# Hybrid RG-LRU / attention / expert-choice step on one core: input weights by column blocks, expert lists from two sorted halves, weight rests in smaller pieces

## What is computed

```python
def _recurrent_mixer(xn, w_in, ...):            # layer 0
    gate, u = jnp.split(xn @ w_in, 2, axis=-1)
    u = _centred_dwconv(u, conv_w, conv_b)
    h = _linear_scan(a_f, b_f, h0_f) + flip(_linear_scan(a_b, b_b, h0_b))
    y = (h * jax.nn.gelu(gate)) @ w_out

def _expert_choice_moe(xn, w_router, w_gate, w_up, w_down):
    aff = jax.nn.softmax(xt @ w_router, axis=-1)
    g, idx = lax.top_k(aff.T, cap)              # cap = 64 latent, 16 context
    xe = xt[idx]
    h = jax.nn.silu(xe @ w_gate) * (xe @ w_up)
    ye = (h @ w_down) * g
    out = zeros.at[idx].add(ye)

# each of the six vectors of a layer (shift, scale, gate for mixer and experts):
m = silu(cond) @ mod_w[layer] + mod_b[layer]
```

## Time and profile before

| | before |
|---|---|
| median of 3 runs (lowest to highest) | 1864.85 us (1864.16 to 1870.14) |
| profiled execution: its own time | 1864.11 us |
| profiled execution: span | 1862.3 us |
| busy share PE, DVE, ACT, POOL | 89%, 33%, 20%, 17% |
| traffic | 524.99 MB, mean 282 GB/s |

### The profile page before, as it was taken

One profiled execution on the slowest core, in us unless ns is written; L12 is line 12 of the kernel. 1 busy time (PEld: TensorE's weight loads), 2 busy tenths in 40 slices (PEclk: granted clock), 3 DMA queues, 4 the chain that ended last, 5 costly groups with the idle time before them and its releaser, 6 DMA issues.

```text
span 1862.3 us, 30729 instructions
## 1 busy us (share of the span) xinstructions
PE 1659.7 (89%) x13351; PEld 771.2 (41%) x13351; DVE 614.3 (33%) x1137; ACT 370.4 (20%) x770; POOL 312.1 (17%) x358
## 2 busy tenths in 40 slices
PE   4799859479999999999879788794799999999997
PEld 0688647123333333332258666472233333333322
DVE  2467675510111121010267567556101111210102
ACT  2377741100000000000151355411000000000000
POOL 1133230210101110110020167301101011101110
PEclk8899979689999999999989899896899999999999
DMA  9400553989999999999920200315899999999993
GB/s 390 146 1 1 214 224 119 410 335 404 382 405 410 399 407 414 401 404 405 336 85 1 96 24 24 137 79 216 313 405 381 403 410 399 405 415 398 407 356 115
DMA packets 57934, 524.99 MB, mean 282 GB/s; under 512 B 12607, under 2 KB 12895, under 8 KB 25038
## 3 DMA queue, kind: packets, MB, share of 16 engines
q1 hardware_dynamic: 48096, 490.62, 64.9%
q0 software_dynamic: 8176, 27.08, 5.2%
q10 hardware_dynamic: 1534, 5.38, 0.7%
HBM read 500.50 MB, written 22.55 MB: 281 GB/s over the span
## 4 chain that ended last, share of the span: by engine, by line
PE 77%; DVE 9%; DMA 5%; ACT 5%; issue 2%; POOL 1%; SPq 0%; DVEq 0%; POOLq 0%; ACTq 0%
PE ps L912 36%; PE ps L916 18%; PE ps L855 6%; PE ps L1170 5%; DMA W<-x_hat,gi_c 2%; DMA ring<-in_mod_w 2%; DMA ring<-in_rg_w_in 1%; PE ps L1218 1%; PE ps L1192 1%; PE ps L1205 1%; PE ps L939 1%; PE ps L1077 1%; PE ps L954 1%; PE ps L759 1%; ACT W L1426 1%
## 5 line engine op out<-in xcount | busy, mean ns | idle before, releaser
L912 PE MATMUL ps<-ring,W 128*32 128x512 f32 x4608 | 552.4, 597 | 4.0 <-issue 2.6
L916 PE MATMUL ps<-ring,W 128*16 128x512 f32 x2304 | 300.2, 593 | 0.0
L912 PEld LDWEIGHTS ps<-ring,W 128*32 128x32 f32 x4608 | 145.9, 110 | 335.1 <-issue 333.0
L1241 ACT ACTIVATE W<-ps 128x512 f32<-128x512 f32 (+5 forms) x137 | 72.0, 542 | 910.5 <-PE ps L954 707.7
L1738 DVE TENSOR_TENSOR W<-ps,amod 128x1024 f32<-128x1024 f32 (+1 forms) x32 | 28.5, 892 | 487.4 <-PE ps L939 366.2
L912 PE MATMUL ps<-over_rows,W 128*32 128x512 f32 x1536 | 182.7, 593 | 0.0
L916 PEld LDWEIGHTS ps<-ring,W 128*16 128x16 f32 x2304 | 67.6, 97 | 177.3 <-issue 177.3
L1747 DVE TENSOR_TENSOR W<-ps,W 128x1024 f32<-128x1024 f32 x16 | 19.6, 1225 | 278.1 <-PE ps L916 278.1
L916 PE MATMUL ps<-over_rows,W 128*16 128x512 f32 x768 | 99.9, 592 | 0.0
L855 PE MATMUL ps<-wo_hl,mo_hi 128*128 128x512 f32 x320 | 89.7, 403 | 5.3 <-DVE mo_lo L1652 5.3
L912 PEld LDWEIGHTS ps<-over_rows,W 128*32 128x32 f32 x1536 | 48.1, 110 | 108.3 <-issue 107.8
(11 more groups left out here) (282 smaller groups left out, 2189.0 us busy)
## 6 DMA issues: line engine op xcount, KB each, us to landing
ring<-in_moe_w_down SPq DMA_DIRECT2D x52, 2048.0 KB, 11.7
ring<-in_moe_w_up SPq DMA_DIRECT2D x48, 2048.0 KB, 13.4
ring<-in_moe_w_gate SPq DMA_DIRECT2D x44, 2048.0 KB, 11.3
ring<-in_mod_w SPq DMA_DIRECT2D x48, 1024.0 KB, 11.3
over_rows<-in_moe_w_gate SPq DMA_DIRECT2D x20, 2048.0 KB, 11.1
over_rows<-in_moe_w_up SPq DMA_DIRECT2D x16, 2048.0 KB, 11.8
over_rows<-in_moe_w_down SPq DMA_DIRECT2D x12, 2048.0 KB, 12.9
ring<-in_rg_w_in SPq DMA_DIRECT2D x8, 1024.0 KB, 27.5
```

The source lines that it names most:

```text
L912: nc.tensor.matmul(ps[q * CG:(q + 1) * CG, bank + n, :], lat(q, k), expert_slots(slots[q // 2], 1)[:, 0, cols], start=(k == 0), stop=(k == ...
L916: mm = nc.tensor.matmul(ps[q * CG:q * CG + CC, bank + 2, :], ctx(a, k), expert_slots(slots[a], 1)[:, 0, h * D + n * 512:h * D + (n + 1) * ...
L1241: nc.scalar.activation(out, in_, ACT.Copy).then_inc(done, n)
```

## The change

- **Opening.** `rg_w_in` is laid out by column blocks, so that slot b holds both column blocks b. SP loads tokens, vectors 1 and 0, then blocks 0 to 3, the small recurrent weights `bd`, and blocks 4 to 7. Vector 2's weights come behind them into slots 0 to 3 and vector 3's into 4 to 7, each slot free once `column_rest` has read it; vector 4's come into slots 0 to 3 once PE has used vector 2's. PE multiplies vectors 2 and 3 together at the last feature block, and 4 behind it; the three are turned together.
- **Mixer output.** PE does the products with high weights of tiles 0 and 1 first, then the weight rests of tile 0, the gate rows, the weight rests of tile 1. In layer 0 ACT makes all 8 high parts between vector 4 and `mo_hi`, and DVE all 8 rests behind the token rests; POOL none.
- **Attention.** POOL splits `at_w_o` in quarters of 128x256: behind every unit from 2 to 34 one high part and one rest.
- **Lists.** The 512 latent tokens are two halves on separate partitions, sorted together in 8 rounds over 256 columns. Merging: the k-th of the first half against the (64-k)-th of the second, the larger of each pair belongs to the best 64. POOL waits for the first 4 lists (indices) instead of 10. An extra exponential of one element stands ahead of the softmax on ACT.

```diff
-MOD_SLOT = {0: 0, 1: 4, 2: 8, 3: 0, 4: 4, 5: 8, 6: 0, 7: 4, 9: 8, 10: 0, 8: 0, 11: 8}
+MOD_SLOT = {0: 8, 1: 4, 2: 0, 3: 4, 4: 0, 5: 8, 6: 0, 7: 4, 9: 8, 10: 0, 8: 0, 11: 8}
...
+        def in_columns(n):
+            return ring[:, n // 2, (1 - n % 2) * D:(2 - n % 2) * D].rearrange("p (k j) -> p k j", k=KB)
...
-            for v in range(3):
+            for v in range(2):
                 load_mod(v, None, None)
-            for s in range(KB):
-                sp.wait_ge(ring_used, used(s // 4, s))
-                put(s, rg_w_in[s * P:(s + 1) * P, :])
+            for b in range(4):
+                put(b, rg_w_in[b])
...
+            for b in range(4, KB):
+                sp.wait_ge(ring_used, used(1, b))
+                put(b, rg_w_in[b])
...
-            for v in (3, 4):
-                load_mod(v, wcol_lo_ok, lambda s: 2 * KB)
+            load_mod(2, wcol_lo_ok, lambda s: 2 * (s + 1))
+            load_mod(3, wcol_lo_ok, lambda s: 2 * (s + 5))
+            load_mod(4, ring_used, lambda s: used(2, s))
...
+            def weight_rests(layer, t, first):
+                toks = slice(t * P, (t + 1) * P)
+                for k in range(KB):
+                    if first:
+                        pe.wait_ge(wo_lo_ok, split_done(layer, k))
+                    for n in range(2):
+                        mm = nc.tensor.matmul(ps[:, 2 * (t % 2) + n, :], mo_hi[:, k, toks], wo_hl[:, k, 1, n * 512:(n + 1) * 512],
+                                              start=False, stop=(k == KB - 1))
+                mm.then_inc(out_mm, 1)
...
+                    if t == 0:
+                        for u in range(2):
+                            main_terms(layer, u, first=(u == 0))
+                        weight_rests(layer, 0, first=True)
+                    elif t == 1:
+                        weight_rests(layer, 1, first=False)
+                    else:
+                        main_terms(layer, t, first=False)
+                        weight_rests(layer, t, first=False)
...
-            modulation(0, 1, 2)
-            pe.wait_ge(mod_read, 3)
+            modulation(0, 1)
+            pe.wait_ge(mod_read, 2)
             turn(0)
...
-                    modulation(3, turn_last=False)
+                    modulation(2, 3, turns=False, turn_last=False)
...
-            out_weights_high(range(KB // 2))
             mod_reads([4])
+            out_weights_high(range(KB))
             mixed_high(0)
-            out_weights_high(range(KB // 2, KB))
...
-                step(v.tensor_copy(tk[0:NE, :], ps[0:NE, 5, :]))
-                step(v.tensor_copy(tk[32:32 + NE, 0:NCTX], ps[0:NE, 3, 0:P]))
+                both = tk[0:HB + NE, 0:NHALF]
+                step(v.tensor_copy(both, ps[0:HB + NE, 5, 0:NHALF]))
...
+                step(v.tensor_copy(merged[:, 0:2], lists[:, :, second]))
+                v.tensor_tensor(merged[:, 2], lists[:, 0, first], merged[:, 0], ALU.is_ge)
+                step(v.tensor_tensor(merged[:, 3], lists[:, 1, first], merged[:, 1], ALU.subtract))
+                v.tensor_tensor(merged[:, 0], lists[:, 0, first], merged[:, 0], ALU.max)
+                step(v.tensor_tensor(merged[:, 3], merged[:, 3], merged[:, 2], ALU.mult))
+                step(v.tensor_tensor(merged[:, 1], merged[:, 1], merged[:, 3], ALU.add))
...
-                pool.wait_ge(route_ok, 10 * (layer + 1))
+                pool.wait_ge(route_ok, 10 * layer + 4)
...
+                if 2 <= u < 4 * KB + 2:
+                    quarter_high(u - 2)
+                if 3 <= u < 4 * KB + 3:
+                    quarter_rest(u - 3)
```

197 lines of the change are left out of this document (106 added, 91 removed).

## The result

| | before | change |
|---|---|---|
| median (lowest to highest, executions) | 1866.37 us (1864.16 to 1870.14, 4) | 1839.38 us (1836.78 to 1842.19, 4) |
| ratio of the times, 95% interval | | 0.9849 (0.9831 to 0.9866) |
| profiled execution: its own time, span | 1864.11, 1862.3 us | 1842.19, 1840.4 us |
| busy share PE, DVE, ACT, POOL | 89%, 33%, 20%, 17% | 91%, 32%, 20%, 17% |

The change takes 27 us off, 1.5%. The page's chain of the changed kernel, by line, reads as the earlier trace rows did: the two lines of the experts lead, now L954 and L958, with the same shares.

What follows compares the result with a forecast made beforehand. The prediction took PE in the two expert stages as the bound, unchanged inside, with gains from starting the experts earlier. Its terms summed to -29.9 on the profiled 1864.1, 1834.2; with 0.7 for the median, 1834.9 us, range 1823 to 1848.

Steps and rivals of the forecast that it cites:

- Step 1: Opening: tokens turned about 10.4 us earlier, PE starts at 51.0 instead of 65.21, -14.2 us; the loop only shifted.
- Step 2: End of the recurrent loop: vector 2's products add 1.5 us; the path behind ACT's last root shortens by 5.0, to 13.1.
- Rival D: Opening: PE waits in the loop for blocks 4 to 7 or vector 4; half the gain lost, 1842; chance 0.1.
- Step 3: Mixer output: a new PE wait ahead of turning tile 0's rows, +3.1 us per layer, +6.2 together.
- Step 4: Lists: shorter operations over 256 columns less the merge's cost, -6.2 us per layer, -12.4 together; bounds +1.0 and -7.5 per layer.
- rival C: Lists: the rounds over 256 columns don't shrink, +2 instead of -12.4, about 1849 us; chance 0.05.
- Rival E: Lists to experts: the first gather still waits for the last token tile's store; half of step 4 lost, 1841; chance 0.07.
- Step 5: Attention: period of units with four key blocks falls from 3.80 to 3.46 us, POOL's operations summed; -6 taken overall.
- rival B: Attention gains nothing or loses up to 8 us, with a period of 3.8 to 4.0: 1841 to 1849; chance 0.2.
- Rival A: Attention clogs: DVE's maximum and statistics meet each POOL operation, 1.89 us more per unit, about 1901; chance 0.03.

Runs made afterwards that it cites:

- e8: The changed kernel with vector 2 in the opening again, its products no longer in the loop, vector 4's weights also earlier: 1847.6 us, 0.9896 of before.
- e5: The changed kernel plus twelve matmuls with overwritten results in PE's wait ahead of the turn of tile 0's rows, both layers: 1837.7 us, 0.9842 of before.
- e6: The changed kernel with all 64 pieces of attention's output weights made ahead of POOL's first division, none in the units: 1872.3 us (one execution).
- e3: The changed kernel with the lists as before (8 rounds over 512 columns, ten copies waited for), keeping the extra exponential: 1851.9 us, 0.9913 of before.
- e2: The changed kernel with attention's weight pieces as before, one 128x1024 high part or rest behind every second unit: 1845.0 us, 0.9871 of before.
- e11: The changed kernel with attention's high parts whole behind every fourth unit and rests still in quarters: 1841.1 us, 0.9857 of before.
- e12: The changed kernel with attention's rests whole behind every fourth unit and high parts still in quarters: 1856.2 us, 0.9944 of before.

## Why the prediction was right, and where it was off

The forecast was 1834.9 in a range from 1823 to 1848; measured 1839.4. As a difference it was 29.9 against 27.0; the other 1.5 is the fourth execution of the kernel before. Term by term, from the two profiles of the change against the one of before:

| step | predicted | measured |
|---|---|---|
| 1 opening | -14.2 | -15.8 and -14.0 |
| 2 end of the loop | +1.5 - 5.0 | -4.2 (189.5 to 185.3 from projection to product) |
| 3 output, both layers | +6.2 | +5.9 + 4.8 = +10.7 |
| 4 lists, both layers | -12.4 | -6.7 - 6.7 = -13.5 |
| 5 attention | -6.0 | -5.4 |
| sum | -29.9 | -26.4 to -28.2 |

**Step 1** was right in its parts. The tokens' turn moved by 12.1 rather than 10.4 (in the second profile by 10.4, so the 1.7 aren't the change's), and the chain behind it took the 13.4 plus one column rest. "The loop itself is only shifted" holds but for the 1.1 us of step 2. Rival D, that PE waits for blocks 4 to 7 or for vector 4, didn't come; the one such wait is 0.63 for vector 4's last slot, and it lies beside ACT's work. e8 showed that 4.4 us of the gain are the layout's. The expert stages kept their length, as the first paragraph of the prediction says: from the second pair's turned rows to the last pair's it is 498.2 us before and 498.8 and 498.2 in the change's profiles.

**Step 2** was right: from ACT's last root to the first product it took 12.8 (13.1 predicted), and DVE's operations 8.0 as at the block before. From the first projection to the root it is 1.1 more than before (1.5 predicted for vector 2's products) and 1.7 more than in e8, which hasn't got them there.

**Step 3 is the term that was mis-sized,** by 4.5 us; the others together gave 1.0 to 2.8 more than forecast, which hid a part of it. The wait itself was right: 30.5 and 30.2 behind the first product, 30.0 predicted, released by DVE's scaling. The sentence "From there on the order is as before and no time is given back" is where it failed: behind the 3.1 us pause the clock was granted at half, and the next tile took 1.6 us longer, in both layers. These 3.2 are most of the 4.5; 0.6 is a longer wait, and 0.7 lies behind the second turn, nearly all of it in layer 0, and was not traced. e5 showed it, by filling the pause, and e8 and e6, where one pause each left the clock at 1.00 and the next tile at 11.8. The row that would have told me was at hand: the first products behind PE's wait at 254.73 took 2.05 for four, twice what I then used per product (0.225).

**Step 4** was right, 23 x 0.26 = 6.0 by the columns (17.6 to 11.5); rival C is out, a maximum takes 0.42. The rows that gave the 0.26 were of two different operations, a maximum of 0.69 and a subtraction of 1.21, so that it held was in part luck. The bounds don't follow from the step's own terms: without the 6.0 it gives -0.2 per layer and not +1.0, and without the merge -8.0 and not -7.5. Rival E is out: e3 costs 11.4 by the ratio, so what is gained in the lists reaches the end. The extra exponential took its 0.20; what it gave is not shown, since no run takes it out alone.

**Step 5** had the right size for a wrong reason. I had summed POOL's operations to a period of 3.46 and took POOL for the bound. With the pieces as measured (cast 0.40, rest 0.73 instead of 0.37 and 0.64) the same sum is 3.58, and the period is 3.56, so the changed kernel alone would have seemed to bear it out. But e6 has 3.48 with none of the pieces, so the quarters, 1.1 us per unit, lie beside other work, all but 0.08 of it. The divisions don't come at an even 3.4 to 3.5 either, but 3.48 and 3.67 apart by turns, and rival B's 3.8 to 4.0 didn't come. What the change removed is the long meeting of DVE's small operation with the 2.37 us rest, which the earlier trace rows shows with 0.91 for an operation of 0.16: e2, e11 and e12 agree on it. In the changed kernel a quarter rest ends at 1106.35 (1105.62 and 0.73), and the small operation starts at 1106.38:

```profile
1105.62 0.73 POOL L721 TENSOR_TENSOR wo_hl<-ring,wo_hl 128x256 fp32r<-128x256 f32 x1
...
1106.38 0.16 DVE L2066 SCALAR_TENSOR_TENSOR stat<-stat,sinks 128x2 f32<-128x2 f32 x1
```

Rival A's condition (that each POOL operation blocks DVE once) didn't arise for that reason. Short meetings are left: in 16 of the 40 units of the changed kernel the small operation takes 0.25 to 0.74. In e6, which has no pieces there, it takes 0.16 in every unit. e12 shows that with whole rests the loss is real. How much of the 5 us is the meeting and how much the granted clock, 0.97 over the 16 units before and 1.00 in the change, was not tried apart. The rule of the Trainium skill (SBUF — State Buffer, "Who interferes with whom") that I had weighed against step 5 agrees with these rows, but as a reason for the gain, not against it.
